# A hybrid decoder trunk on one core: another place for the powers, the weights' copies and the third value chunk

## The chip, the cores and the metric

The kernel runs on one core of a Trainium2 chip. The metric is the device time of one execution in microseconds. The core has five engines that run their own instruction streams and meet only at semaphores: TensorE (PE, with its weight loads as PEld), VectorE (DVE), ScalarE (ACT), GpSimd (POOL) and SyncE (SP). Each engine executes its stream in the order in which it is written; a wait stands for all that is behind it on that engine.

## The reference, cut to what matters

One inference step of a two-layer trunk for a prompt of 512 tokens and 8 sample tokens. Around the change lies layer 0's mixer. It has three computations side by side:

```python
# samples: attention over 4096 paged past positions each, k and v gathered by page table
a = softmax(q1 @ k1 * s + bias) - lam * softmax(q2 @ k2 * s + bias);  out = a @ v
# prompt: the same with a causal mask, 4 heads, blocks of 128 queries
# prompt and samples: gated linear attention, in chunks of C = 16 tokens
att = where(causal, qe @ ke.T, 0);  o = att @ v + qe @ S
S = exp(b_last) * S + kd.T @ v
# each head's output
o = o * rsqrt(mean(o * o) + eps) * g          # times silu(gate) for the linear heads
```

Then the output projection, an MLP, layer 1 (a gated recurrent block) and its MLP follow, all dense products.

## The kernel before

**Stages.** 13 chunks of the input projection; then 16 attention units (head, query block) of the prompt; then 8 GLA units (token block `tb`, pair of heads `hp`), numbered `u` in the loops of lines 1455 (VectorE), 965 (ScalarE) and 1923 (TensorE); then the projections and MLPs in `products` (line 1710).

**The paged cache.** The samples' keys and values come in 128 gathers (64 for k, 64 for v) of 1 MB, all issued by GpSimd with `indirect_dma_start` (line 705) into a ring of six buffers `KV`. `ORDER` fixes their order: 28 of k, then `v k v` per attention unit, then `k v` three times per GLA unit 0 to 5, so that key steps 44 + 3u to 46 + 3u and value chunks 32 + 3u to 34 + 3u belong to GLA unit u (units 6 and 7 have key steps 62 and 63 only). Before GpSimd issues gather i it goes through what belongs to gather i - 6, whose buffer it takes: it makes the product of the key step one ahead (`pool_product`), and waits in `release` until that buffer's user is done.

**A key step.** Half of it is VectorE's (`k_first`, lines 1247 and 1249: product and reduction into `SC`), half is GpSimd's product into the one buffer `PROD[:, 1]` (line 638), which VectorE reduces in `k_second` (line 1235). `k_chunks` on VectorE does `k_second(n - 1)` and then `k_first(n)`; the product of step n waits for `k_second(n - 1)`:

```python
            if n >= 1:
                po.wait_ge(prod1_used, n)
```

At the last step of a sample (n % 8 == 7) its own `k_second(n)` follows at once.

**A value chunk.** TensorE (`v_chunks`, line 1870) multiplies it with `PM`, a copy of the softmax weights that GpSimd makes (`weights`, line 651; the first also clears the tile, line 646). One copy serves four chunks: chunk n needs copy n // 4.

**The norm of an output.** When the outputs of unit u are in `OT`, VectorE clamps them (`clamp`, line 1415), ScalarE sums the squares, GpSimd takes the power -1/2 (`power`, lines 662 and 666), VectorE multiplies (`inverse_norm`, line 1421), ScalarE makes a diagonal of it (line 911), TensorE multiplies with it (`normalise`, line 1885) and ScalarE evicts (line 917). In the GLA loop all that from the power on stands in the next unit: unit u normalises the outputs of u - 1, counted as 15 + u. `POWERS_BEFORE_K` says before the product of which key step a power stands on GpSimd, `POWER_BEHIND_V` behind the release of which value chunk.

**A GLA unit.** TensorE: transpose (line 1927), masks' products (line 1933, which wait for the clamp), a value chunk, updates (line 1945), a second chunk, the sample's outer product, `normalise`, a third chunk, outputs (lines 1961 and 1966), which wait for the eviction of `normalise`. VectorE: a key step, masks (line 1462), eight state updates (line 1467), `inverse_norm`, a key step, `state_write` (line 1392), a key step, the clamp.

Of the kernel before, what the change touches and what calls it, by code (L numbers as in the profile page):

```python
# [112 lines left out]
def trunk(nc, ctx, a, o):  # L113
# [56 lines left out]
    RING = len(KV)  # L170
# [120 lines left out]
    def sem(name):  # L291
        return ctx.enter_context(nc.semaphore(name))
# [128 lines left out]
    v_used = sem("v_used")  # L421
# [75 lines left out]
    ORDER = load_order()  # L497
# [130 lines left out]
    def _(po):  # L628
# [25 lines left out]
        K_IN_UNITS = sum(UNIT_STEPS) + 2 * 11 + sum(PRE_STEPS)  # L654
        POWERS_BEFORE_K = {K_IN_UNITS: (14, 15), **{K_IN_UNITS + 3 * u + 1: (15 + u,) for u in range(1, 7)}}
        POWER_BEHIND_V = {**{2 * u + 1: u - 1 for u in range(1, 15)}, 53: 22, 57: 23}

# [10 lines left out]
        def release(i):  # L668
            kind, n = ORDER[i]
            if kind == "k":  # L670
                po.wait_ge(k_used, n + 1)
                po.wait_ge(prod1_ready, n + 1)
            else:
                po.wait_ge(v_used, n + 1)
                if n in POWER_BEHIND_V:
                    power(POWER_BEHIND_V[n])

        def weights_behind(i):

            kind, n = ORDER[i]  # L680
            if kind == "v":
                if n == 0:
                    weights(0)
                if n % 8 == 1:
                    weights(2 * (n // 8) + 1)
                if n % 8 == 7 and n < 63:
                    weights(2 * (n // 8) + 2)

        AHEAD = 1
        for i in range(LOADS + RING):  # L690
            if i >= RING:
                weights_behind(i - RING)
                for ahead in range(0 if i == RING else AHEAD, AHEAD + 1):
# [9 lines left out]
            if i < LOADS:  # L703
                kind, n = ORDER[i]
# [436 lines left out]
    def _(ve):  # L1141
# [313 lines left out]
        for u, (tb, hp) in enumerate(GLA_UNITS):  # L1455
            steps = GLA_STEPS[u]
# [7 lines left out]
            for n in range(8):  # L1464
                if n % 4 == 0:
                    ve.wait_ge(u_done, 2 * u + n // 4 + 1)
                V.scalar_tensor_tensor(ST[:, hp, state(tb, n + 1)], ST[:, hp, state(tb, n)], DECC[:, hp, 8 * tb + n:8 * tb + n + 1],  # L1467
                                       update(n, slice(0, P)), ALU.mult, ALU.add).then_inc(st_ready, 1)
                ve.wait_ge(st_ready, 8 * u + n + 1)
            if u:  # L1470
                inverse_norm(15 + u)
            k_chunks(min(max(steps - 1, 0), 1))
            state_write(u)
# [188 lines left out]
    def _(pe):  # L1662
# [260 lines left out]
        for u, (tb, hp) in enumerate(GLA_UNITS):  # L1923
# [26 lines left out]
            state_values(u)  # L1950
            pe.wait_ge(st_ready, 8 * u + 8)
            if u:
                normalise(15 + u)
            v_chunks(34 + 3 * u, 1)
            if u:
                pe.wait_ge(nev_done, outputs_done(16 + u))
# [128 lines left out]
```

## Time and profile before

| what | value |
|---|---|
| median of 3 runs | 1643.63 us (1642.11 to 1647.47) |
| the profiled execution, its own time | 1642.11 us |
| its span in the trace | 1640.3 us |
| PE, PEld busy | 88%, 79% |
| DVE, ACT, POOL busy | 56%, 30%, 21% |
| attention units (from the first value chunk) | 232 to 366 us |
| GLA units, transpose of the first to the last chunk's end | 381 to 543 us |

The profile is of one execution. The page gives shares over the whole span, and the stages differ: before 554 us the transfers, VectorE and GpSimd work most of the time, behind it TensorE nearly alone. So stretches are read by themselves: a window gives each engine's busy time in it, the granted clock of TensorE as a share of 2.4 GHz (PEclk) and the mean busy share of the 16 DMA engines. A timeline row gives start and duration, and in brackets how long the engine had been idle and what released it.

### The profile page before, as it was taken

To read this page: it belongs to the slowest core of one execution; us is meant where nothing else is said; L and a number is where in the kernel's file an instruction comes from. 1 tells how busy PE (TensorE), PEld (TensorE's weight loads), DVE (VectorE), ACT (ScalarE), POOL (GpSimd) and SP (SyncE) were. 2 spreads that over 40 slices of the span, in tenths; PEclk is the share of its full clock that TensorE was granted. 3 is DMA by queue.
4 is the path that set the end of the run, shared out by engine and by line. 5 is a ranking of instruction groups with operands and counts; after the bars stand their busy time and mean duration, and the time that the engine had idled before them with its cause. 6 is when DMAs were issued, how large, how long until landed. Compare 5 with 4: busy or idle time off the path is not lost.

```text
span 1640.3 us, 25826 instructions
## 1 busy us (share of the span) xinstructions
PE 1441.9 (88%) x11004; PEld 1291.3 (79%) x11004; DVE 912.9 (56%) x1157; ACT 499.9 (30%) x800; POOL 339.6 (21%) x270
## 2 busy tenths in 40 slices
PE   4999957767777788999999998799979999999995
PEld 3999823434333687999999997799969999999994
DVE  2498978766885527435353444769536434353433
ACT  3322354431322323212121223437243212121222
POOL 1085768865675000000000000002000000000000
PEclk9999979887777799999999999899989999999998
DMA  8477699996889431232322321112212232222311
GB/s 296 134 257 243 237 326 379 376 384 240 330 312 346 168 103 52 81 100 82 99 95 86 103 78 52 54 60 71 92 38 78 81 101 89 92 92 89 103 53 52
DMA packets 127892, 250.32 MB, mean 153 GB/s; under 512 B 5267, under 2 KB 108455, under 8 KB 111136
## 3 DMA queue, kind: packets, MB, share of 16 engines
q0 software_dynamic: 18432, 134.23, 21.5%
q1 hardware_dynamic: 101984, 105.00, 19.8%
q10 hardware_dynamic: 7368, 9.50, 1.8%
q8 instruction: 87, 1.43, 0.4%
q14 instruction: 21, 0.17, 0.0%
HBM read 241.04 MB, written 7.73 MB: 152 GB/s over the span
## 4 chain that ended last, share of the span: by engine, by line
PE 74%; DVE 13%; POOL 4%; ACT 4%; DMA 2%; issue 2%; ACTq 0%; another core or an unknown queue 0%; DVEq 0%; POOLq 0%
PE PS L1710 62%; PE PS L1695 3%; POOL PROD L638 3%; DMA KV<-in_cache_v,CIDX 2%; PE PS L1870 2%; DVE SC L1235 1%; DVE RS L1188 1%; POOL KV L705 1%; DVE TMP L1214 1%; PE PS L2003 1%; DVE ST L1467 1%; PE PS L1945 1%; DVE X L1218 1%; DVE ACC L1619 1%; DMA XSIN<-in_x_sample 1%
## 5 line engine op out<-in xcount | busy, mean ns | idle before, releaser
L1710 PE MATMUL PS<-H_hi,W_hi 128*128 128x260 f32 x1936 | 397.6, 287 | 23.2 <-DVE H_lo L1184 13.2
L1710 PE MATMUL PS<-H_hi,W_lo 128*128 128x260 f32 x1936 | 394.1, 286 | 0.0
L1710 PE MATMUL PS<-H_lo,W_hi 128*128 128x260 f32 x1936 | 393.4, 285 | 0.0
L1710 PEld LDWEIGHTS PS<-H_hi,W_hi 128*128 128x128 f32 x1936 | 304.1, 192 | 27.7 <-issue 20.6
L1710 PEld LDWEIGHTS PS<-H_hi,W_lo 128*128 128x128 f32 x1936 | 302.6, 191 | 0.0
L1710 PEld LDWEIGHTS PS<-H_lo,W_hi 128*128 128x128 f32 x1936 | 302.0, 191 | 0.0
L1179 DVE TENSOR_TENSOR W_lo<-RAW,W_hi 128x2048 fp32r<-128x2048 f32 x94 | 217.4, 2313 | 130.5 <-ACT W_hi L775 129.9
L775 ACT ACTIVATE W_hi<-RAW 128x2048 fp32r<-128x2048 f32 x94 | 179.5, 1909 | 278.0 <-PE PS L1710 277.7
L1710 PE MATMUL PS<-U_hi,W_lo 128*128 128x260 f32 x1024 | 206.4, 283 | 0.0
L1710 PE MATMUL PS<-U_lo,W_hi 128*128 128x260 f32 x1024 | 206.0, 283 | 0.0
L1710 PE MATMUL PS<-U_hi,W_hi 128*128 128x260 f32 x1024 | 206.0, 282 | 0.0
L638 POOL TENSOR_TENSOR PROD<-KV,QB 128x1024 f32<-128x1024 f32 x64 | 151.8, 2372 | 123.4 <-DVE SC L1235 91.7
L1710 PEld LDWEIGHTS PS<-U_hi,W_hi 128*128 128x128 f32 x1024 | 157.9, 188 | 0.0
L1710 PEld LDWEIGHTS PS<-U_hi,W_lo 128*128 128x128 f32 x1024 | 157.9, 188 | 0.0
L1710 PEld LDWEIGHTS PS<-U_lo,W_hi 128*128 128x128 f32 x1024 | 157.4, 188 | 0.0
L1574 DVE TENSOR_TENSOR ACC<-ACC,PS 128x520 f32<-128x520 f32 x64 | 44.6, 697 | 200.3 <-PE PS L1710 200.3
L1037 ACT ACTIVATE UF<-SQ 128x520 f32<-128x520 f32 x64 | 40.8, 638 | 279.9 <-DVE SQ L1564 279.9
L721 POOL TENSOR_TENSOR INP<-GX,ACC 128x520 f32<-128x520 f32 x7 | 14.5, 2081 | 505.6 <-ACT GX L1106 499.2
L1870 PE MATMUL PS<-KV,PM 128*32 128x512 f32 x512 | 87.0, 767 | 27.8 <-DMA KV<-in_cache_v,CIDX 15.7
L1564 DVE SCALAR_TENSOR_TENSOR SQ<-PS,RS 128x520 f32<-128x520 f32 x64 | 44.8, 700 | 112.9 <-PE PS L1710 112.9
L1695 PE MATMUL PS<-SQ,ONES 128*128 128x260 f32 x256 | 72.9, 442 | 33.3 <-ACT SQ L797 33.3
L1695 PEld LDWEIGHTS PS<-SQ,ONES 128*128 128x128 f32 x256 | 51.9, 218 | 53.3 <-issue 29.0
(287 smaller groups left out, 1509.1 us busy)
## 6 DMA issues: line engine op xcount, KB each, us to landing
RAW<-in_w_up SPq DMA_DIRECT2D x32, 1024.0 KB
RAW<-in_w_down SPq DMA_DIRECT2D x32, 1024.0 KB
RAW<-in_w_in_even SPq DMA_DIRECT2D x13, 1024.0 KB
RAW<-in_w_in_odd SPq DMA_DIRECT2D x8, 1024.0 KB
RAW<-in_w_out_odd SPq DMA_DIRECT2D x5, 1024.0 KB
RAW<-in_w_out_even SPq DMA_DIRECT2D x4, 1024.0 KB
x_saved<-X ACTq DMA_DIRECT2D x1, 2080.0 KB, 6.4
X<-x_saved SPq DMA_DIRECT2D x1, 2080.0 KB, 9.4
```

What stands on the lines that cost most here:

```text
L638: nc.gpsimd.tensor_tensor(PROD[:, 1], KV[i % RING][:, 2:4, :], QB[:, None, b % 2, :].to_broadcast([P, 2, 512]), ALU.mult).then_inc(prod1_r ...
L705: po.indirect_dma_start(KV[i % RING].rearrange("p n f -> p (n f)"), None, cache[kind], bass.IndirectOffsetOnAxis(ap=CIDX[:, n:n + 1], axis ...
L775: A(W_hi[:, ch.slot], RAW[:, ch.slot], ACT.Copy).then_inc(w_hi_ready, 1)
L1037: A(UF[:, i], RL[:, i], ACT.Square).then_inc(uf_ready, 1)
L1179: V.tensor_tensor(W_lo[:, ch.slot], RAW[:, ch.slot], W_hi[:, ch.slot].bitcast(F32), ALU.subtract).then_inc(w_lo_ready, 1)
L1188: V.reciprocal(RS[:, 1], RS[:, 0]).then_inc(inverse_ready, 1)
L1214: t = V.scalar_tensor_tensor(TMP[:, q], ACC[:, kt + q], VEC[:, gain + kt + q:gain + kt + q + 1], RS[:, 1], ALU.mult, ALU.mult)
L1564: V.scalar_tensor_tensor(pair(RL[:, i]), banks(ch.par[i]), 0.0, pair(RS[:, 1]), ALU.max, ALU.mult).then_inc(banks_free[ch.par[i]], 1)
L1574: V.tensor_tensor(pair(ACC[:, m]), pair(ACC[:, m]), banks(ch.par[i]), ALU.add).then_inc(banks_free[ch.par[i]], 1)
L1695: t = MM_(PS[:, 4 + i, 0:HALF], ONES[:], SQ[:, kt % 2, half], start=kt == 0, stop=kt == KT - 1)
L1710: t = MM_(PS[:, 2 * ch.par[i] + j, 0:HALF], w[:, ch.slot, k, cols], x[:, k, half], start=k == 0 and n == 0, stop=k == KT - 1 and n == 2)
L1870: t = MM_(PS[32 * pos:32 * pos + 32, 4, :], PM[:, part % 2, at:at + 32], KV[i % RING][:, pos, :], start=n % 32 == 0, stop=n % 32 == 31)
```

## The change

On GpSimd the weights' copies move from ahead of the product that is one step ahead to behind it, directly ahead of the wait for the value chunk (`weights_behind` goes into `release`). The powers of the GLA units move from before key step 45 + 3u to before key step 46 + 3u (`3 * u + 2`), and the last ones behind other value chunks: 21 from key step 63 to chunk 51, 22 from chunk 53 to chunk 54. On VectorE the middle key step of a GLA unit comes before `inverse_norm`. On TensorE the third value chunk of a GLA unit comes before `normalise`. No instruction is added or removed.

```diff
--- before.py
+++ after.py
@@ -652,8 +652,8 @@
                                   SC[b % SLOTS][:, :, 16 * half:16 * half + 16].rearrange("p j n -> p n j")).then_inc(pm_ready, 1)
 
         K_IN_UNITS = sum(UNIT_STEPS) + 2 * 11 + sum(PRE_STEPS)
-        POWERS_BEFORE_K = {K_IN_UNITS: (14, 15), **{K_IN_UNITS + 3 * u + 1: (15 + u,) for u in range(1, 7)}}
-        POWER_BEHIND_V = {**{2 * u + 1: u - 1 for u in range(1, 15)}, 53: 22, 57: 23}
+        POWERS_BEFORE_K = {K_IN_UNITS: (14, 15), **{K_IN_UNITS + 3 * u + 2: (15 + u,) for u in range(1, 6)}}
+        POWER_BEHIND_V = {**{2 * u + 1: u - 1 for u in range(1, 15)}, 51: 21, 54: 22, 57: 23}
 
         def power(u):
 
@@ -671,25 +671,19 @@
                 po.wait_ge(k_used, n + 1)
                 po.wait_ge(prod1_ready, n + 1)
             else:
-                po.wait_ge(v_used, n + 1)
-                if n in POWER_BEHIND_V:
-                    power(POWER_BEHIND_V[n])
-
-        def weights_behind(i):
-
-            kind, n = ORDER[i]
-            if kind == "v":
                 if n == 0:
                     weights(0)
                 if n % 8 == 1:
                     weights(2 * (n // 8) + 1)
                 if n % 8 == 7 and n < 63:
                     weights(2 * (n // 8) + 2)
+                po.wait_ge(v_used, n + 1)
+                if n in POWER_BEHIND_V:
+                    power(POWER_BEHIND_V[n])
 
         AHEAD = 1
         for i in range(LOADS + RING):
             if i >= RING:
-                weights_behind(i - RING)
                 for ahead in range(0 if i == RING else AHEAD, AHEAD + 1):
                     j = i - RING + ahead
                     if j < LOADS and ORDER[j][0] == "k":
@@ -1467,9 +1461,9 @@
                 V.scalar_tensor_tensor(ST[:, hp, state(tb, n + 1)], ST[:, hp, state(tb, n)], DECC[:, hp, 8 * tb + n:8 * tb + n + 1],
                                        update(n, slice(0, P)), ALU.mult, ALU.add).then_inc(st_ready, 1)
                 ve.wait_ge(st_ready, 8 * u + n + 1)
+            k_chunks(min(max(steps - 1, 0), 1))
             if u:
                 inverse_norm(15 + u)
-            k_chunks(min(max(steps - 1, 0), 1))
             state_write(u)
             slot(GLA_SLOT + 2 * u + 1)
             k_chunks(max(steps - 2, 0))
@@ -1949,10 +1943,9 @@
             v_chunks(33 + 3 * u, 1)
             state_values(u)
             pe.wait_ge(st_ready, 8 * u + 8)
+            v_chunks(34 + 3 * u, 1)
             if u:
                 normalise(15 + u)
-            v_chunks(34 + 3 * u, 1)
-            if u:
                 pe.wait_ge(nev_done, outputs_done(16 + u))
             for par in range(2):
                 h, rows = 2 * hp + par, slice(64 * par, 64 * par + 64)
```

Line 655's dictionary holds, before: `{44: (14, 15), 48: (16,), 51: (17,), 54: (18,), 57: (19,), 60: (20,), 63: (21,)}`; after: `{44: (14, 15), 49: (16,), 52: (17,), 55: (18,), 58: (19,), 61: (20,)}`. GpSimd's stream in GLA unit 2, with the wait for a buffer's user left out: before, power 17, product 51, gathers v41 and k54, copy 10, product 52, gathers v42 and k55; after, product 51, gathers v41 and k54, power 17, product 52, copy 10, gathers v42 and k55. The copies that end up behind a product are 0, 8, 9, 10, 11, 12 and 13.

## Rows read from the trace of the kernel before

**Rows 1.** The chain that ended last: start us, us, what.
```profile
553.99 49.02 PE PS L1710 x384
```

**Rows 2.** Busy time by window: attention's end, then two units of line 1927.
```profile
310.00:350.00 40.00, 33.23 (x189) 15.05 (x188) 32.58 (x52) 16.76 (x56) 30.95 (x32) 0.86 0.96 386
...
417.20:438.05 20.85, 13.89 (x108) 7.13 (x105) 16.53 (x27) 8.51 (x23) 16.02 (x15) 0.69 0.85 312
438.05:453.03 14.98, 11.26 (x107) 5.72 (x103) 12.24 (x23) 5.04 (x19) 9.27 (x9) 0.89 0.78 299
```

**Rows 3.** Waits from 372 to 556 us: total, times, longest.
```profile
POOL PROD L638 <- DVE SC L1235: 35.7, 12, 14.7
...
DVE NRS L1421 <- POOL NRS L666: 4.4, 1, 4.4
```

**Rows 4.** Timeline of unit 2: start us, us, engine, line, tiles, idle before.
```profile
424.80 0.72 POOL L666 TENSOR_TENSOR NRS<-NRT,EPSC 128x2 f32<-128x2 f32 x1
...
426.72 1.21 DVE L1235 TENSOR_REDUCE SC<-PROD 128x16 f32<-128x1024 f32 x1
...
428.08 2.36 POOL L638 TENSOR_TENSOR PROD<-KV,QB 128x1024 f32<-128x1024 f32 x1 [2.56 <-DVE SC L1235]
...
430.35 1.44 DVE L1392 SCALAR_TENSOR_TENSOR S<-PS,KSS,S 64x128 f32<-64x128 f32 x4
...
431.93 0.94 POOL L705 DMA_INDIRECT KV<-in_cache_k,CIDX  x1 [0.30 <-issue]
...
432.88 0.41 POOL L651 COPY PM<-SC 128x128 f32<-128x128 f32 x1
...
433.43 1.94 PE L1870 MATMUL PS<-KV,PM 128*32 128x512 f32 x8 [5.29 <-POOL PM L651]
...
435.30 0.80 PE L1961 MATMUL PS<-GVT,ATTM 128*128 128x128 f32 x2
...
439.21 0.42 DVE L1415 TENSOR_SCALAR OTC<-PS 128x256 f32<-128x256 f32 x1 [3.33 <-ACT OT L983]
```

**Rows 5.** Timeline of units 1, 3, 6 and 7, single steps.
```profile
411.80 1.93 PE L1870 MATMUL PS<-KV,PM 128*32 128x512 f32 x8 [0.79 <-DMA KV<-in_cache_v,CIDX]
...
447.90 1.21 DVE L1235 TENSOR_REDUCE SC<-PROD 128x16 f32<-128x1024 f32 x1
...
503.61 1.21 DVE L1235 TENSOR_REDUCE SC<-PROD 128x16 f32<-128x1024 f32 x1
...
508.55 0.53 PE L1961 MATMUL PS<-GVT,ATTM 128*128 128x128 f32 x2
...
522.14 0.16 DVE L1421 SCALAR_TENSOR_TENSOR NRS<-NSQ,NRS 128x2 f32<-128x2 f32 x1
...
522.88 0.69 PE L1885 MATMUL PS<-NDG,OT 128*128 128x128 f32 x4 [0.62 <-ACT NDG L911]
...
524.50 0.49 PE L1961 MATMUL PS<-GVT,ATTM 128*128 128x128 f32 x2
```

**Rows 6.** Timeline of unit 0, single steps.
```profile
381.73 1.93 PE L1870 MATMUL PS<-KV,PM 128*32 128x512 f32 x8
...
383.59 1.98 PE L1945 MATMUL PS<-GVT,KDM 128*64 128x128 f32 x16
...
384.08 2.35 POOL L638 TENSOR_TENSOR PROD<-KV,QB 128x1024 f32<-128x1024 f32 x1 [14.68 <-DVE SC L1235]
...
386.75 3.02 DVE L1467 SCALAR_TENSOR_TENSOR ST<-ST,DECC,PS 128x128 f32<-128x128 f32 x8
```

**Rows 7.** Timeline of the first attention unit, single steps.
```profile
230.62 1.02 POOL L646 MEMSET PM<- 128x1072 f32 x1
...
232.24 1.94 PE L1870 MATMUL PS<-KV,PM 128*32 128x512 f32 x8 [1.74 <-POOL PM L651]
...
234.72 2.37 POOL L638 TENSOR_TENSOR PROD<-KV,QB 128x1024 f32<-128x1024 f32 x1 [2.62 <-DVE SC L1235]
...
237.24 1.02 POOL L705 DMA_INDIRECT KV<-in_cache_v,CIDX  x1 [0.15 <-POOL PROD L638]
```

## The prediction

> **What bounds the kernel now.** I read the page first: the program's end is set by TensorE for most of the span, so an edit counts only if it lengthens or shortens a stretch in which the dense products (line 1710) wait for something. The edit touches only the stretch before the output projection, which follows at 553.99 us of the span [rows 1]. So I cut that stretch into its units with the windows view, one window from each transpose of line 1927 to the next. In a unit no engine is full: in the unit of 20.85 us VectorE works 16.53, GpSimd 16.02, TensorE 13.89 and the transfers 0.85 of the time; in the next, of 14.98 us, it is 12.24, 9.27, 11.26 and 0.78 [rows 2]. Work of 12 to 17 us on each of four resources fills units of 15 to 22 us: the stage is bound by the order in which they hand over to one another, and a reordering can cost much without adding any work. The waits view says which hand-over matters: GpSimd's product waits 35.7 us for VectorE's second reduction of the step before, and VectorE waits for GpSimd's power once only, 4.4 us [rows 3]. The timeline of one unit then gives each step of the loop; in it the third chunk of values waits 5.29 us for the copy of the weights [rows 4].
>
> **The change part by part.** It adds and removes no instruction. It moves three things: on GpSimd the power of a unit goes behind one more product and pair of gathers, and the weights' copy goes behind the product ahead of it; on VectorE the middle key step goes ahead of `inverse_norm`; on TensorE the third chunk of values goes ahead of `normalise`. What matters is who waits for whom in the new order.
>
> *The power.* Take the unit of rows 4 and call t0 the end of its middle `k_second` (426.72 + 1.21 = 427.93). Now the power is over at 425.52 (424.80 + 0.72), and `inverse_norm` runs just ahead of 426.72 without waiting. After the change VectorE does the key step first and comes to `inverse_norm` where it now comes to the state write, 2.42 us after t0 (430.35). GpSimd may start its product only 0.15 after t0 (428.08), then takes 2.36 for it, issues two gathers and is free at 432.87, 4.95 after t0; only there will the power stand. It is the 0.72 and a small operation ahead of it, which I take at 0.3 (the copy, which is larger, takes 0.41): 1.0 us. So `inverse_norm` runs 6.1 us after t0, and VectorE stands for 3.7 us. The stall isn't covered: behind it are the state write (1.44) and the third `k_second`, which alone lets GpSimd start its next product. That product starts now at t0 + 5.6 at the earliest; it will start at about 6.1 + 0.1 + 1.5 + 1.2 + 0.15 = t0 + 9.1.
>
> *The rest of the loop.* From `inverse_norm` over the diagonal, the normalising matmuls and their eviction to the outputs it is 2.4 us (522.14 to 524.50), of which 1.6 are from those matmuls on (522.88) [rows 5]. The outputs' start to the clamp is 3.9 us (435.30 to 439.21), and from the clamp over the next unit's masks, first chunk, updates and states to its middle `k_second` 8.7 (439.21 to 447.90), which takes 1.2. So t0 to the next t0 is 6.1 + 2.4 + 3.9 + 8.7 + 1.2 = 22.3 us, if no transfer is later than that. That `k_second` stands now at 447.90 and, three units on, at 503.61: 18.6 us a unit [rows 5]. **Units 3, 4 and 5 cost 3.7 us each, 11.1 together.** In unit 1 the outputs now stand straight behind the third chunk, which waits for its gather (411.80, for 1.93). That gather goes out 0.5 later still than the unit, since the copy of this unit (0.41) stands behind a product as well; behind the chunk there will be matmuls and eviction of `normalise` (1.6), and I add 0.3 for the Silu that ScalarE does ahead of it: **2.4 us.** In unit 6 the power stands behind the product of step 63, its gathers and chunk 51, so `inverse_norm` is at t0 + 6.1 there too (VectorE, which has another `k_second` ahead, stands 2.3), and the outputs at t0 + 8.5; they are now at 508.55, 3.7 after its t0 of 504.82. That is 4.8, and 2.3 if the outputs wait for something else now: **4.0 us**, near the upper one, since TensorE has nothing else there. Unit 7: the power waits for chunk 54 instead of 53, 0 to 1.1 us (a chunk at the upper clock level): **0.6 us.**
>
> *The weights.* The chunks of values of one part cannot start before the part's copy (0.41). In the unit of rows 4 the copy stands at 432.88 and the third chunk (433.43) already waits for it. After the change, ahead of it stand the power and the next product, and that product waits for the third `k_second`: t0 + 9.1, with a row sum 0.4 more, + 2.36 for the product, and the copy is over at t0 + 12.4, at 440.3. The chunk starts 7 us later than now, and since `normalise` will stand behind it on TensorE, the outputs follow 1.9 + 1.6 us after it: t0 + 15.9 where a unit with the stall alone has them at 8.5. The next t0 comes at t0 + 15.9 + 3.9 + 8.7 + 1.2 = 29.7, against 21.2 now (447.90 minus 426.72). **Unit 2 costs 8.5 us.** In unit 5 the copy stands behind a product as well, but there it only moves a chunk that ends before the power, so I add nothing. In unit 0, the first chunk of values, 381.73 now, goes ahead of all update matmuls; its copy gets behind the product at 384.08, which ends at 386.44. The chunk starts at 387.0 in place of 381.73 (5.3 late), the updates behind it at 389.0, and the states after the first half of them (1.98), at 391.0 and not at 386.75 [rows 6]: **4.3 us.** Ahead of that, the power of unit 14 no longer stands behind a copy, **0.5 us less**. At the first unit of attention the same happens with the memset (1.02) and the first copy: the product runs at 234.72 to 237.09, so chunk 0 starts at 238.7, not 232.24, and the gather that waits for it goes out at about 240.8, not 237.24 [rows 7]. 6.5 us late on TensorE, 3.5 on the transfers. From 310 to 350 us the transfers are 0.96 busy [rows 2], so they can win back little; of the bounds 0 (all won back) and 6.5 I take **3.0 us**, near the gather's delay.
>
> Sum: 3.0 - 0.5 + 4.3 + 2.4 + 8.5 + 11.1 + 4.0 + 0.6 = 33.4 us. Against the profiled execution's own 1642.1 us (span 1640.3) this is 1675.5. The median shown, 1643.6, is 1.5 higher; a median run would be at 1677, and I take 1676 between them.
>
> *The clock.* In the short unit, at a granted clock of 0.89, most matmuls run at the upper of the two levels (2.4 GHz); at 0.69 many run at the lower (1.2 GHz) [rows 2], and a chunk of values then takes 1.94 [rows 4]. If TensorE waits longer per unit, it may stay at the lower level in units that are now at the upper. By rows, at most 3 us in unit 3 and 1 in others; it widens the upper end by 6 us and isn't in the sum. The Trainium skill ("TensorE: Matmul & The Clock Gate", Part 1: The HAM clock gate) says that the throttled state is the default and that activity releases it; the trace agrees, with 0.69 in the unit in which TensorE is busy 13.89 of 20.85 us and 0.89 in that with 11.26 of 14.98. By the rule the sum would lie up to those 6 us higher.
>
> **The rivals.** (a) *The transfers are the bound and swallow most of it.* The gather engine keeps a rate, the ring of six buffers stays full, and a late instruction only eats waiting. For it: 0.96 busy in attention. Against it: 0.85 and 0.78 in these units, and each gather is issued behind the very product that now starts 3.5 us later. If half of the delays in units 0 to 7 (30.9 us) were swallowed, and all of attention's, it would be 1642.1 + 15.5 - 0.5 = 1657. (b) *Faster.* `k_second` goes ahead of `inverse_norm` and the product ahead of the copy, so GpSimd is let go earlier, and the third chunk no longer waits for the diagonal; its buffer is refilled sooner. The gain per unit is at most 0.16 (`inverse_norm`), 0.5 (copy) and 1.2 (`normalise`, where the values have landed): some 5 us over the stage, 1637. It decides if the power is there when VectorE asks for it: GpSimd would have to be 3.7 us further ahead than t0 allows, that is to have begun the product before the `k_second` that frees its buffer. I see no row for that. (c) *Nothing moves:* the stalls just replace other waits of the same engines; VectorE idles 4.3 us in the unit of 20.85, about one stall. But its idle time there is the wait for the outputs at the unit's end, which gets later too. 1642. (d) *More than the sum:* each delay also runs at the lower clock, and attention's 6.5 us stays whole: 33.4 + 3.5 + 6, about 1685.
> The Trainium skill ("DMA: Bandwidth & Descriptors", Anatomy of one DMA) gives for one gather of 1 MiB through GpSimd's path an estimate of 2.0 us plus its bytes at 436 GB/s, 4.4 us. No row here shows a gather by itself, and if that held for the later-spaced gathers, the 0.5 us in unit 1 would vanish, 33.4 becoming 32.9; nothing else here uses it.
>
> **How the numbers follow.** Forecast (1664 to 1683) 0.67, (a) 0.14, (d) 0.10, (c) 0.04, (b) 0.05. A measurement of this kernel can tell about 0.3%, 5 us, from no change. Slower by more than that: 0.91; within: 0.04; faster: 0.05. The range takes in (a) and (d): 1655 to 1689.
>
> **What would show it.** In the trace after: VectorE waiting for GpSimd's power (line 666) at `inverse_norm` in five or six units, some 3.5 us each, where it is one wait of 4.4 us now; the third `k_second` of a unit 5 us or more behind the middle one's key step; in unit 2 a chunk of values waiting over 7 us for PM; in unit 0 TensorE waiting about 5 us for PM; at attention's start about 6 us for the same; the units from transpose to transpose at 22 us in place of 18.7; nothing changed from the output projection on but its start. I am wrong if the power stands ready at `inverse_norm`, or if the units keep their length although VectorE stalls, which would say that the transfers or TensorE set it.

## The result: 2.6% slower, 42 us

Timed side by side on one chip, the changed kernel takes 1686.57 us (median of 4 runs, 1682.45 to 1688.24) and the one before 1642.87 (4 runs, 1641.93 to 1647.47). The ratio is 1.0256 with a 95% interval of 1.0229 to 1.0285: 42.1 us slower, 37.6 to 46.8. (This ratio is an estimate over all runs and not the quotient of the two medians, which lie 43.7 us apart.) I had forecast 1676.0, that is 33.4 us more; the range of 1655 to 1689 holds the time, the narrower 1664 to 1683 of the forecast itself does not. The profiled execution of the changed kernel took 1682.64 us with a span of 1680.8, 40.5 us more span than before. Sums below are made against those 40.5 us.

In the changed kernel the lines behind 692 have numbers lower by 6, and behind 1955 by 7 (the chunks of values are 1864, the dense products 1704, the outputs 1954). In the runs further down they are off by one or a few as well.

First the page of the kernel after, its span and busy times:

```profile
span 1680.8 us, 25820 instructions
...
PE 1455.7 (87%) x11004; PEld 1298.4 (77%) x11004; DVE 913.1 (54%) x1157; ACT 500.1 (30%) x800; POOL 339.4 (20%) x270
```

VectorE, ScalarE and GpSimd are as busy as before within 0.3 us each (912.9, 499.9 and 339.6 us there): no work came in. TensorE has 13.8 us more than before's 1441.9 although it runs the same matmuls. I come back to that.

The chain that ended last says that the whole loss lies ahead of the output projection, whose products start 40.6 us later than in [rows 1]. Columns are start us, us, what:

```profile
564.75 10.44 DMA out_gla_prompt<-ST
...
594.57 48.98 PE PS L1704 x384
```

The waits view of the kernel after, from 372 to 596 us, answers to [rows 3]; columns are total us, times, longest:

```profile
POOL PROD L638 <- DVE SC L1229: 64.3, 17, 14.7
...
DVE NRS L1415 <- POOL NRS L666: 24.3, 8, 4.7
...
PE PS L1864 <- POOL PM L651: 20.7, 3, 13.5
```

VectorE's one wait of 4.4 us for the power, which is that for the last power, behind unit 7, has become eight, 24.3 us together: that one is still there with 4.7, units 1 to 6 have 1.15, 3.68, 4.06, 3.67, 4.60 and 2.16, and unit 7 has 0.33. GpSimd's product, which waited 35.7 us for VectorE, waits 64.3: the stall of the one is handed on to the other. And the three chunks of values that waited 7.6 us for a copy of the weights before wait 20.7.

The timeline of unit 2 after shows both in one unit. It answers to [rows 4]; a number in brackets is the idle time of that engine ahead of the instruction, and who ended it:

```profile
440.18 1.22 DVE L1229 TENSOR_REDUCE SC<-PROD 128x16 f32<-128x1024 f32 x1
...
441.54 2.35 POOL L638 TENSOR_TENSOR PROD<-KV,QB 128x1024 f32<-128x1024 f32 x1 [3.41 <-DVE SC L1229]
...
446.62 0.73 POOL L666 TENSOR_TENSOR NRS<-NRT,EPSC 128x2 f32<-128x2 f32 x1
447.45 0.16 DVE L1415 SCALAR_TENSOR_TENSOR NRS<-NSQ,NRS 128x2 f32<-128x2 f32 x1 [3.68 <-POOL NRS L666]
...
450.69 2.35 POOL L638 TENSOR_TENSOR PROD<-KV,QB 128x1024 f32<-128x1024 f32 x1 [3.35 <-DVE SC L1229]
...
452.99 0.39 POOL L651 COPY PM<-SC 128x128 f32<-128x128 f32 x1
...
453.52 1.94 PE L1864 MATMUL PS<-KV,PM 128*32 128x512 f32 x8 [13.55 <-POOL PM L651]
...
455.39 1.23 PE L1879 MATMUL PS<-NDG,OT 128*128 128x128 f32 x4
...
457.33 0.49 PE L1954 MATMUL PS<-GVT,ATTM 128*128 128x128 f32 x2 [0.71 <-ACT PJ L911]
```

Read it from t0 = 440.18 + 1.22 = 441.40, the end of the middle `k_second`. GpSimd's product, which that step lets go, and its two gathers keep it until 446.3; the power follows; `inverse_norm` runs at t0 + 6.05 after a stall of 3.68. The next product starts at t0 + 9.3, the copy ends at t0 + 12.0, and TensorE, which has stood for 13.55 us, starts the chunk at t0 + 12.1 and the outputs at t0 + 15.9. The prediction had 6.1 for `inverse_norm`, 3.7 for the stall, 9.1 for the product, 12.4 for the end of the copy and 15.9 for the outputs.

To add up the loss I cut both traces at the masks' products (line 1933 before, 1927 after), at whose start the outputs of the unit before are over. Two of the units, first before and then after. Columns are the window, its length, busy us (instructions) of TensorE, its weight load, VectorE, ScalarE, GpSimd, then the granted clock, the transfers' share and GB/s:

```profile
399.30:418.30 19.00, 15.58 (x107) 7.32 (x107) 16.94 (x30) 5.29 (x17) 14.17 (x12) 0.68 0.98 373
...
476.20:494.80 18.60, 14.80 (x105) 7.68 (x105) 16.45 (x28) 6.28 (x21) 14.03 (x13) 0.68 0.87 324
```

```profile
409.40:432.30 22.90, 19.84 (x107) 8.92 (x107) 16.87 (x30) 5.13 (x15) 15.74 (x13) 0.50 0.83 318
...
504.90:529.90 25.00, 17.80 (x105) 8.91 (x106) 16.50 (x28) 6.30 (x22) 15.13 (x13) 0.57 0.73 258
```

These are units 1 and 5. Such cuts for all of the stage give what each part lost, beside its term of the forecast. "Before" and "after" are lengths in us. One trace is one execution, so the last column gives the same stretch in other traces: those of the six runs below that move one copy, one clearing or one gather of the kernel before (`e5` to `e8`, `e10`, `e11`), each where it leaves the stretch alone.

| stretch | before | after | more | forecast | unchanged, elsewhere |
|---|---|---|---|---|---|
| start of chunk 0 (after: less its added wait) | 232.2 | 231.6 | -0.7 | none | 229.2 to 233.7 |
| chunk 0 to unit 0 (after: with the added wait, 6.4) | 148.8 | 155.4 | +6.6 | +3.0, -0.5 | 147.9 to 150.0 |
| unit 0 | 18.3 | 22.5 | +4.3 | +4.3 | 18.3 to 19.0 |
| unit 1 | 19.0 | 22.8 | +3.8 | +2.4 | 19.4 to 21.7 |
| unit 2 | 21.5 | 28.2 | +6.7 | +8.5 | 20.7 to 21.8 |
| unit 3 | 18.7 | 22.0 | +3.3 | +3.7 | 18.2 to 18.7 |
| unit 4 | 17.6 | 22.4 | +4.8 | +3.7 | 17.1 to 17.8 |
| unit 5 | 18.7 | 25.0 | +6.3 | +3.7 | 18.5 to 19.0 |
| unit 6 | 19.2 | 22.1 | +2.9 | +4.0 | 15.3 to 16.2 |
| unit 7 to the output projection | 39.9 | 42.5 | +2.6 | +0.6 | 38.2 to 40.0 |
| sum | | | +40.6 | +33.4 | |

The first line is no effect of the change, which does nothing ahead of chunk 0 but delay it: that start varies by more from run to run. Unit 6 of the kernel before is 3 us longer in this trace than in any of the others. ScalarE's second copy of its outputs stands there for something that the profile can't name:

```profile
513.19 0.28 ACT L983 ACTIVATE OT<-PS 128x128 f32<-128x128 f32 x1 [1.94 <-remote]
```

Against the other traces unit 6 loses about 6 us, not 2.9, and unit 1 about 2.5, not 3.8. The terms that are most short are attention, unit 5, what follows unit 6 and, by this better base, unit 6 itself.

What follows unit 6 has a wait that the kernel before doesn't have in this trace. ScalarE sends the last states out (`out_gla_prompt`) and may begin the split of the output projection's input (`H_hi`) only when they have landed. First before, then after:

```profile
534.15 2.18 ACT L998 ACTIVATE H_hi<-PJ 128x512 fp32r<-128x512 f32 x4
```

```profile
575.21 2.19 ACT L992 ACTIVATE H_hi<-PJ 128x512 fp32r<-128x512 f32 x4 [2.89 <-DMA out_gla_prompt<-ST]
```

That is the transfer of 10.44 us in the chain above, and its 2.89 us are about the 2.6 of the table.

### The profile page after: what moved, and what is told of

It reads as the page before. It is cut to its first block, busy times and chain, and to the rows that moved or that the text cites. A ratio compares the mean times of both kernels' runs of the same rounds, so it can differ in the third digit from the quotient of the medians.

```text
span 1680.8 us, 25820 instructions
## 1 busy us (share of the span) xinstructions
PE 1455.7 (87%) x11004; PEld 1298.4 (77%) x11004; DVE 913.1 (54%) x1157; ACT 500.1 (30%) x800; POOL 339.4 (20%) x270
## 3 DMA queue, kind: packets, MB, share of 16 engines
q1 hardware_dynamic: 101984, 105.00, 19.4%
## 4 chain that ended last, share of the span: by engine, by line
PE 74%; DVE 13%; ACT 4%; POOL 4%; issue 2%; DMA 2%; ACTq 0%; DVEq 0%; POOLq 0%
PE PS L1704 61%; PE PS L1689 3%; POOL PROD L638 3%; PE PS L1864 2%; DVE SC L1229 2%; DVE RS L1182 1%; PE PS L1939 1%; DVE TMP L1208 1%; PE PS L1996 1%; POOL KV L699 1%; DVE ST L1461 1%; DVE X L1212 1%; DVE ACC L1613 1%; PE PS L1959 1%; DMA out_gla_prompt<-ST 1%
## 5 line engine op out<-in xcount | busy, mean ns | idle before, releaser
L1864 PE MATMUL PS<-KV,PM 128*32 128x512 f32 x512 | 90.7, 797 | 45.1 <-POOL PM L651 28.9
```

What stands on the lines that cost most here:

```text
L1864: t = MM_(PS[32 * pos:32 * pos + 32, 4, :], PM[:, part % 2, at:at + 32], KV[i % RING][:, pos, :], start=n % 32 == 0, stop=n % 32 == 31)
```

## The experiments

My theory after the result: the three moves cost what the hand-over loop says, the first copy costs its whole delay since nothing wins back transfer time that is lost in attention, and the copy of unit 5, which I had put at nothing, costs something. The rivals: the transfers take part of it up (then attention's share is under 6), the chunk order is what hurts, or the lower clock carries what is missing. "Ratio" is against the kernel before in the same batch, with a 95% interval; each is turned into us with that batch's median of before (1642.9, 1640.0 or 1639.3; the batches ran on different chips). A difference of medians can be some us off from it: 9.6 in place of 12.2 for `e3_chunk`, 24.6 in place of 26.4 for `e9_early_powers`. Lengths of units are from the one trace of each run, cut as above.

### The three moves, each alone

**All copies late, all else as before (`e1_copies`).**

```diff
             else:
+                weights_behind(i, True)
                 po.wait_ge(v_used, n + 1)
...
-                weights_behind(i - RING)
+                weights_behind(i - RING, False)
```

> Only the weights' copies go behind the product; powers, VectorE and TensorE keep their order. Theory (the loop of hand-overs sets the stage, late work ahead of a value chunk is paid in full): copy 0 costs 6.5 us, copy 8 costs 3.8, copy 10 about 3 (it stands behind product 52, 433.5 to 435.9, so the chunk starts at 436.4 and not 433.4), copy 12 about 3: some 16 us, 1659. Rival (the gathers' rate sets it, late instructions are mostly swallowed): under 6 us.

Measured: 1658.82 us, ratio 1.0091 (1.0071 to 1.0112), 15.0 us more, beside the theory's 16. Its unit 2, TensorE:

```profile
453.14 1.94 PE L1871 MATMUL PS<-KV,PM 128*32 128x512 f32 x8 [8.28 <-POOL PM L651]
455.01 0.80 PE L1962 MATMUL PS<-GVT,ATTM 128*128 128x128 f32 x2
```

The chunk's wait is 8.28 instead of 5.29 us [rows 4], and the outputs stand straight behind it.

**All powers late (`e2_powers`).** The two tables of the change and VectorE's order; TensorE and the copies as before.

```diff
-        POWERS_BEFORE_K = {K_IN_UNITS: (14, 15), **{K_IN_UNITS + 3 * u + 1: (15 + u,) for u in range(1, 7)}}
-        POWER_BEHIND_V = {**{2 * u + 1: u - 1 for u in range(1, 15)}, 53: 22, 57: 23}
+        POWERS_BEFORE_K = {K_IN_UNITS: (14, 15), **{K_IN_UNITS + 3 * u + 2: (15 + u,) for u in range(1, 6)}}
+        POWER_BEHIND_V = {**{2 * u + 1: u - 1 for u in range(1, 15)}, 51: 21, 54: 22, 57: 23}
...
+            k_chunks(min(max(steps - 1, 0), 1))
             if u:
                 inverse_norm(15 + u)
-            k_chunks(min(max(steps - 1, 0), 1))
```

> Only the powers go one product and two gathers later and VectorE's middle key step goes ahead of inverse_norm (the two can't be parted: the late power alone would wait for a key step that stands behind it). Theory: inverse_norm waits 3.7 us in units 2 to 5, 1 in unit 1, 2.3 in unit 6, and TensorE's third chunk, still behind normalise, adds 1 us a unit: 20 to 25 us, 1662 to 1668. Rival (gathers): under 10 us.

Measured: 1673.1 us, ratio 1.0185 (1.0164 to 1.0207), 30.4 us more (26.9 to 34.0): above the 20 to 25 that I expected. Its waits view from 372 to 596 us:

```profile
POOL PROD L638 <- DVE SC L1235: 56.0, 15, 14.7
...
DVE NRS L1421 <- POOL NRS L666: 24.2, 8, 4.5
```

The stalls for the power are those of the whole change (24.2 against 24.3 us), so the moved power makes them. VectorE's order, moved with it here, doesn't: `e9_early_powers` below has that order with early powers, and none of these stalls.

**The third chunk ahead of `normalise` (`e3_chunk`).**

```diff
+            v_chunks(34 + 3 * u, 1)
             if u:
                 normalise(15 + u)
-            v_chunks(34 + 3 * u, 1)
-            if u:
                 pe.wait_ge(nev_done, outputs_done(16 + u))
```

> Only TensorE's third chunk goes ahead of normalise. Theory: the norm is not the late one before, the chunk is (its gather or its copy), so the order costs the matmuls and the eviction of normalise behind the chunk, 1 to 1.6 us in the four or five units in which the chunk waits for a gather or copy: plus 4 to 7 us, 1647 to 1650. Rival (the buffer is let go earlier and that is what counts): minus 2 to 5 us.

Measured: 1652.51 us (6 runs, 1645.63 to 1657.13), ratio 1.0074 (1.0054 to 1.0093), 12.2 us more (8.9 to 15.3). The rival that expected a gain falls, and the loss is larger than the theory had. The profiled execution is the fastest of the six (1645.63), so its timeline can't show the median's loss; it shows the mechanism. Unit 2, TensorE and the clamp:

```profile
434.31 1.93 PE L1870 MATMUL PS<-KV,PM 128*32 128x512 f32 x8 [6.38 <-POOL PM L651]
436.17 1.22 PE L1885 MATMUL PS<-NDG,OT 128*128 128x128 f32 x4
...
438.11 0.80 PE L1960 MATMUL PS<-GVT,ATTM 128*128 128x128 f32 x2 [0.72 <-ACT PJ L917]
...
442.17 0.42 DVE L1415 TENSOR_SCALAR OTC<-PS 128x256 f32<-128x256 f32 x1 [5.40 <-ACT OT L983]
```

`normalise` could run while TensorE waits for the copy. Behind the chunk, it and ScalarE's eviction lie on the way to the outputs: 438.11 - 436.17 = 1.9 us.

**The power and the chunk together (`e4_no_copies`),** the change without its copies.

> The change without its copies: powers, VectorE's and TensorE's order as in the kernel after, copies ahead of the product as before. Theory (parts add up, but the order of chunk and normalise costs nothing once the norm is late): 42 us of the whole less 6.5 for copy 0, 4.3 for copy 8, 4.8 for copy 10 in the presence of the late power (8.5 less 3.7) and 2.5 for copy 12: 24 us, 1667. Rival (copies are cheap, the powers carry nearly all): 35 us, 1678.

Measured: 1671.91 us, ratio 1.0176 (1.0159 to 1.0193), 28.9 us more. That lies between the theory's 24 and the rival's 35. With the late power the chunk order costs nothing more that could be measured (30.4 without it), whereas alone it costs 12.2. Where the power is late, the chunk can run in the time in which TensorE waits for it anyway. And 28.9 + 15.0 (the copies alone) = 43.9, beside 42.1 for the whole: copies on one side, power and chunk on the other, add up within their intervals.

**The change with early powers (`e9_early_powers`):** the two tables put back, everything else as in the change.

> The kernel after with the powers alone back where they were; copies, VectorE's and TensorE's order stay changed. Theory (the late power is the stall, not VectorE's new order): inverse_norm waits for no power in units 1 to 6, and what is left is the copies' 15 and the chunk order's 10 us: plus 25, 1665 to 1668. Rival (VectorE's order itself costs, the norm coming one key step later): over 32, 1675.

Measured: 1663.93 us, ratio 1.0161 (1.0132 to 1.019), 26.4 us more. That is the theory's 25. VectorE waits for a power once again, 4.4 us, as before. Undoing the power's move gives back 16 us, though that move alone costs 30. So "what the power costs" has no single value: taken first it is 30, taken last it is 16. The order in which the parts are taken says why: the copies cost 15.0, the chunk order (with VectorE's) on top of them 26.4 - 15.0 = 11.4, about what it costs alone, and the power on top of both 15.7. A late power hides the chunk order, so whichever comes first has the whole of the shared part.

### The copies one by one

Each runs one copy in the changed place, all else as before.

```diff
+        LATE = (0,)          # or (8,), (10,), (12,)
...
+                if part is not None and (part in LATE) == late:
+                    weights(part)
```

> Only copy 0 and the clearing of its tile go behind product 28. Theory (nothing of it is won back, since attention's next product waits for VectorE, which waits for TensorE): the first chunk 6.5 us late and the whole 6.5 later, 1649.5. What the prediction took (the transfers win part of it back): 3.0. Rival (the gathers' rate alone counts): 3.6, the delay of the next gather.

> Only copy 8 goes behind product 44. Theory: unit 0 is 4.3 us longer and power 14 0.5 us earlier, 3.8 in all, 1646.7. Rival (transfers, which are only half busy in this unit, catch up in unit 1): under 1 us.

> Only copy 10 goes behind product 52. Theory: the third chunk of unit 2 starts at 436.4 and not 433.4 and unit 2 is 3 us longer: 1646. In the kernel after, with the late power, the same copy cost more because its product waits for the third k_second. Rival: the copy is no longer the late one here, 0.

> Only copy 12 goes behind product 60. The prediction took nothing for it. By the trace of the kernel after, the chunk behind it waited 5.85 us for it, and by the order of the loop the outer product and the state write stand behind that chunk: plus 3 us, 1643 to 1646 beside a kernel before of 1640 to 1643. Rival (the prediction's): 0.

| copy | of | us | ratio | more | chunk's wait, before | with this copy late | its unit: elsewhere, here, in `e1` |
|---|---|---|---|---|---|---|---|
| 0 | attention | 1646.86 | 1.0040 (1.0022 to 1.0057) | 6.6 | 1.74 | 8.10 | see below |
| 8 | unit 0 | 1644.91 | 1.0031 (1.0012 to 1.0051) | 5.1 | none | 5.07 | 18.3 to 19.0, 22.2, 22.3 |
| 10 | unit 2 | 1643.68 | 1.0025 (1.0009 to 1.0041) | 4.1 | 5.29 | 8.29 | 20.7 to 21.8, 24.8, 24.7 |
| 12 | unit 5 | 1646.45 | 1.0043 (1.0027 to 1.0059) | 7.0 | 1.00 | 5.95 | 18.5 to 19.0, 23.4, 23.3 |

The two columns of waits are the idle time in brackets at that chunk. What is added to it (6.4, 5.1, 3.0 and 5.0 us) is near the price for each of the four. The four come to 22.8 us singly and 15.0 together, but each has an interval of some 3 us to either side, so this doesn't show that they hide one another. The traces say that they don't: each unit is as long with its copy late alone as in `e1_copies`, where all are late.

*Copy 0* costs 6.6 us. The prediction gave 3.0, with 6.5 as the upper bound. *Copy 12* costs 7.0 where the prediction gave nothing, which is more than the 3 I expected of this run too (its interval is 4.4 to 9.7). Its unit 5, first in the kernel before and then with only this copy late:

```profile
482.80 0.40 POOL L651 COPY PM<-SC 128x128 f32<-128x128 f32 x1
...
483.35 1.06 PE L1870 MATMUL PS<-KV,PM 128*32 128x512 f32 x8 [1.00 <-POOL PM L651]
484.35 1.12 PE L1847 MATMUL PS<-GVTOK,CONST 8*128 8x512 f32 x2
...
488.30 1.94 PE L1870 MATMUL PS<-KV,PM 128*32 128x512 f32 x8 [1.88 <-DMA KV<-in_cache_v,CIDX]
...
494.83 0.89 PE L1933 MATMUL PS<-QE,KE 64*128 64x128 f32 x4 [0.68 <-DVE OTC L1415]
```

```profile
489.98 2.35 POOL L638 TENSOR_TENSOR PROD<-KV,QB 128x1024 f32<-128x1024 f32 x1 [2.68 <-DVE SC L1236]
...
492.28 0.39 POOL L651 COPY PM<-SC 128x128 f32<-128x128 f32 x1
...
492.81 1.94 PE L1871 MATMUL PS<-KV,PM 128*32 128x512 f32 x8 [5.95 <-POOL PM L651]
494.68 2.07 PE L1848 MATMUL PS<-GVTOK,CONST 8*128 8x512 f32 x2
...
496.86 0.34 DVE L1393 SCALAR_TENSOR_TENSOR S<-PS,KSS,S 64x128 f32<-64x128 f32 x1 [4.64 <-PE PS L1848]
...
503.02 0.58 PE L1934 MATMUL PS<-QE,KE 64*128 64x128 f32 x4 [0.79 <-DVE OTC L1416]
```

The chunk isn't the last of its kind here: behind it on TensorE is the product of line 1848, which VectorE's state write waits for (4.64 us), with the next `k_second` behind that. I had looked only at the chunk's end against the power's. The two matmul groups also take longer: behind the 5.95 us of idle time they run at the lower level of the clock, 1.94 and 2.07 us in place of 1.06 and 1.12. It is tempting to add these 1.83 us to the added wait of 4.95 and find the 7.0. The trace doesn't bear that out: unit 5 is 23.4 us long in it and 18.7 in the kernel before, 4.8 us more (23.45 - 18.67) and not 6.8. From this chunk to the masks of the next unit it is 11.5 us before (494.83 - 483.35) and 10.2 here (503.02 - 492.81), since the third chunk waited 1.88 us for its gather before and doesn't now. So the copy costs its added wait, and the rest of the 7.0 is within the run's interval.

### Can attention win transfers back?

**GpSimd 3.7 us late from one gather on (`e11_gather_late`).** GpSimd clears a spare tile 18 times ahead of the gather of chunk 4, the one that copy 0 delays; copy 0, power and orders stay.

```diff
+        DUMMIES = 18
...
+                if (kind, n) == ("v", 4):
+                    for j in range(DUMMIES):
+                        nc.gpsimd.memset(DUM[:, :], 0.0).then_inc(pm_zeroed, 1)
+                        po.wait_ge(pm_zeroed, j + 2)
```

> The kernel before with 18 small clearings of a spare tile on GpSimd ahead of the gather of chunk 4, the first behind product 28: they should take some 2 to 5 us (read from the trace), so that gather and all behind it on GpSimd goes out that much later, while chunk 0 starts in time. Theory (in attention the hand-overs set the pace, but the gathers at 0.94 to 0.99 busy leave no room for winning back): between half and all of the delay stays at the end. Rival (the gathers wait in the ring anyway): nothing stays.

GpSimd's timeline, the delay and the gather behind it:

```profile
238.47 3.69 POOL L709 MEMSET DUM<- 128x64 f32 x18
242.43 1.01 POOL L711 DMA_INDIRECT KV<-in_cache_v,CIDX  x1 [0.27 <-POOL DUM L709]
```

Measured: 1644.52 us, ratio 1.0027 (1.0011 to 1.0043), 4.4 us more, 1.8 to 7.1. Against the delay of 3.7 us this leaves nothing that was won back, though the interval allows half of it. The traces are sharper. From the start of chunk 0 to the masks of unit 0 it is 147.9 to 150.1 us in the seven traces that have copy 0 early and all gathers in time (148.9 on average), 147.8 to 150.2 in the five in which chunk 0 starts 6.4 us late (148.6), and 152.7 in this one. So the first 6.4 us are there at the end in full, and so are these 3.7. The windows of the first attention stretch and of a later one, before and then after:

```profile
228.00:248.00 20.00, 14.26 (x82) 6.36 (x83) 16.85 (x27) 8.34 (x26) 15.30 (x16) 0.81 0.99 345
```

```profile
228.00:248.00 20.00, 11.15 (x60) 4.76 (x60) 10.54 (x17) 7.25 (x23) 9.41 (x10) 0.65 0.82 284
...
310.00:350.00 40.00, 31.33 (x173) 14.31 (x169) 31.72 (x50) 16.73 (x58) 30.80 (x33) 0.83 0.98 380
```

The transfers fall from 0.99 to 0.82 busy while the first chunk is awaited, and from 310 us on they are at 0.98 as they were at 0.96 [rows 2]. So they are nearly full either way and have little room to make up for a pause. That this is the cause isn't shown apart from the hand-overs: in `e11_gather_late` the product behind is late as well, 10.1 us behind the one ahead of it and not 6.5, and no run delays the transfers alone.

### Does the clock carry the rest?

TensorE is busy 118.4 us in the units after and 109.3 before (sum of the eight windows up to 15 us into unit 7), for the same matmuls, at a granted clock of 0.50 to 0.68 in units 1 to 6 against 0.68 to 0.79. In unit 1 it is 19.84 of 22.90 us at 0.50 against 15.58 of 19.00 at 0.68. Part of that is spread between executions: in the six runs that move one thing the same sum is 106.1 to 113.5 us, and unit 1, untouched, is at 0.50 in `e8_copy12` too. Still, 118.4 is above all of them, and this looks like rival (d). To test it I gave TensorE idle matmuls in the changed kernel, into a part of PSUM that nothing reads in this stage, ahead of and behind the third chunk of units 2, 3, 4 and 6 (**`e12_warm`**, 50 in all):

```diff
+            warm({2: 20, 3: 5, 4: 5}.get(u, 0))
             v_chunks(34 + 3 * u, 1)
+            warm({3: 4, 4: 4, 6: 12}.get(u, 0))
...
+                MM_(PS[:, 3, 0:P], IDENT, IDENT, start=True, stop=True)
```

> The kernel after with idle matmuls (identity by identity into a free bank, results unused) where TensorE stood waiting in units 2, 3, 4 and 6: 20 and 5 and 5 ahead of the third chunk, 4, 4 and 12 behind it. They give TensorE work only, none of it needed. Theory (the 7 us that the parts' sum leaves open are matmuls at the lower clock): the granted clock of those units rises from 0.65 towards 0.9, and the time falls by 4 to 8 us against the kernel after, to 1679 to 1683. Rival (the clock plays no part on the path): same or, where the added matmuls outlast the wait, 1 to 4 us slower, 1687 to 1691.

Measured: 1684.87 us, ratio 1.0283 (1.026 to 1.0306), beside 1.0256 (1.0229 to 1.0285) for the change itself: no gain, at best a tie, and between what the theory and the rival had. The trace says that this wasn't the test that I meant. TensorE in its unit 2, the idle matmuls (with two records for each), the third chunk and the outputs:

```profile
442.38 4.73 PE L1884 MATMUL PS<-CONST 128*128 128x128 f32 x40
455.11 1.93 PE L1864 MATMUL PS<-KV,PM 128*32 128x512 f32 x8 [8.00 <-POOL PM L651]
...
458.91 0.79 PE L1961 MATMUL PS<-GVT,ATTM 128*128 128x128 f32 x2 [0.71 <-ACT PJ L911]
```

The idle matmuls are over 8.00 us before the chunk, which runs at the lower level of the clock all the same; so do the outputs, 0.79 us where the change alone had 0.49. In units 3 and 4 TensorE stands 3.62 and 2.58 us between the last idle matmul and `normalise`, and the outputs are at 0.79 us too. By unit, with the granted clock of each:

| unit | idle matmuls | the change: us, clock | with them: us, clock |
|---|---|---|---|
| 0 | none | 22.5, 0.65 | 22.3, 0.73 |
| 1 | none | 22.8, 0.50 | 24.4, 0.57 |
| 2 | 20 | 28.2, 0.68 | 30.3, 0.67 |
| 3 | 9 | 22.0, 0.66 | 22.5, 0.73 |
| 4 | 9 | 22.4, 0.65 | 22.1, 0.73 |
| 5 | none | 25.0, 0.57 | 24.4, 0.64 |
| 6 | 12 | 22.1, 0.65 | 21.7, 0.74 |

The units without idle matmuls gained 0.07 to 0.08 as well, and unit 1, which has none, is 1.6 us longer. So neither the clock nor the times can be put down to the idle matmuls. The Trainium skill ("TensorE: Matmul & The Clock Gate", Part 1: The HAM clock gate) has activity release the throttle; this run neither bears that out nor speaks against it.

Two other runs say more. The windows of `e2_powers` and then of `e4_no_copies`, from the masks of unit 0 to 15 us into unit 7:

```profile
380.80:556.60 175.80, 111.62 (x839) 55.89 (x842) 122.96 (x206) 43.62 (x148) 99.26 (x85) 0.69 0.73 265
```

```profile
384.10:557.60 173.50, 121.10 (x839) 61.96 (x842) 122.93 (x206) 43.70 (x148) 99.44 (x85) 0.63 0.73 268
```

The second has TensorE busy 9.5 us longer for the same matmuls, at 0.63 and not 0.69, and is no longer for it: 1671.91 us beside 1673.10. What it is busy longer it stands less, 52.4 and not 64.2 us. One place where the clock is on the path is the outputs: from their start to the next unit's masks it is 4.6 us in the units of the changed kernel in which they run at the lower level and 3.1 in its unit 2, where they run at the upper one (460.47 - 457.33). But five of the eight units have them at the lower level after the change, and five before it. So I find no sign that the clock carries much of the loss; what its share is stays open.

### The other way round

If copy 0 with its clearing costs 6.6 us behind a product and copy 10 costs 4.1, the two waits that the kernel before still has for them, 1.74 [rows 7] and 5.29 us [rows 4], might be had as well. **`e10_early`** changes the kernel before: the tile is cleared ahead of product 25, and copy 10 goes out behind chunk 38 instead of 39.

```diff
+            if n == 25:
+                po.wait_ge(tiles_done, first_tile(C_OUT0))
+                nc.gpsimd.memset(PM[:], 0.0).then_inc(pm_zeroed, 1)
...
-                po.wait_ge(tiles_done, first_tile(C_OUT0))
-                nc.gpsimd.memset(PM[:], 0.0).then_inc(pm_zeroed, 1)
...
-                if n % 8 == 7 and n < 63:
+                if n == 38:
+                    weights(10)
+                if n % 8 == 7 and n < 63 and n != 39:
```

> The kernel before, pushed the other way: copy 10 goes one chunk earlier (behind chunk 38 and ahead of product 51, where GpSimd waited 2.6 us for VectorE), and the tile is cleared ahead of product 25, where GpSimd waited 6.7 us. Theory (lateness of a copy ahead of a waiting chunk counts in full, and so does earliness): 3 to 4 us in unit 2 and 1.0 at attention's start, 4 to 5 us faster. Rival (another wait takes the place, the gather or the third key step): under 1 us.

Measured: 1635.34 us (12 runs, 1632.8 to 1639.0), the kernel before beside it 1639.32 (20 runs), ratio 0.9975 (0.9961 to 0.9989), 4.1 us faster than before (1.8 to 6.4). Chunk 0, the copy of unit 2 and its third chunk:

```profile
227.76 1.94 PE L1873 MATMUL PS<-KV,PM 128*32 128x512 f32 x8 [0.69 <-POOL PM L652]
...
424.61 0.42 POOL L652 COPY PM<-SC 128x128 f32<-128x128 f32 x1
...
430.53 1.93 PE L1873 MATMUL PS<-KV,PM 128*32 128x512 f32 x8 [2.17 <-DMA KV<-in_cache_v,CIDX]
...
437.02 0.89 PE L1936 MATMUL PS<-QE,KE 64*128 64x128 f32 x4 [0.64 <-DVE OTC L1418]
```

The copy is over 5.5 us before the chunk, which now waits for its gather (2.17 us). Unit 2 runs from 418.74 to 437.02, 18.3 us instead of 21.5; that is 3.2 of the 4.1. Whether the clearing adds its 1 us isn't shown: chunk 0 waits 1.05 us less, but from it to unit 0 this trace has 152.0 us, more than in any of the twelve traces counted above. This version beats both kernels, by a margin that is small but measured.

## Why the prediction was right, and where it was short

The direction, the stage and the mechanism were right, and the total was 42.1 (37.6 to 46.8) against 33.4 us. The signs that it named are in the trace: the stalls at `inverse_norm`, 13.55 us for PM in unit 2, 5.07 in unit 0, 6.4 more at attention's start, units of 22 us, and a loss at the output projection (40.6) that is the loss of the whole (40.5).

- **The power: right in its working.** `inverse_norm` at t0 + 6.05 (6.1 said) after a stall of 3.68 (3.7); five of the units 1 to 6 stall 2.16 to 4.60 us, unit 1 less (1.15). The units 3, 4 and 6 are 22.0 to 22.4 us long where I had 22.3. What they lose depends on the base. My 18.6 was a mean over three units, and unit 4 was 17.6, so it loses 4.8.
- **Unit 6: under-priced, and by luck it doesn't look so.** I read its 4.0 from the one trace of the kernel before, in which it is 19.2 us; six other traces have 15.3 to 16.2, so its loss is about 6 us.
- **Unit 0: right,** 4.3 us, with the chunk starting after 5.07 us of idle (5.3 said). With copy 8 alone late the unit is 22.2 us, 3.2 to 3.9 more than in traces that leave it alone.
- **Unit 2: right in its steps, 1.8 too much in size** (6.7 against 8.5). The outputs came at t0 + 15.9 as said. I then added the way on to the next t0 and took 21.2 off as the unit before. From masks to masks it was 21.5 to 28.2.
- **Attention: "near the gather's delay" failed,** the step that gave 3.0 between 0 and 6.5. It is 6.6, by the trace and by copy 0 alone. I counted the delay of a gather (3.5) as the cost, since the transfers are the full resource. But the chunk is 6.4 late, and GpSimd's next product waits for VectorE, which waits for TensorE, so the gathers behind the first pair are as late as the chunk: that product starts at 247.22 after and at 241.19 before. The 0.5 for the power of unit 14 is too small to be seen in this stretch.
- **Unit 5: "so I add nothing" failed.** The copy lengthens the unit by 4.8 us alone, and the unit loses 6.3 instead of 3.7. What is behind the chunk is an outer product that the state write needs, then the third chunk, then `normalise`. After the change the third chunk ends 1.7 us behind `inverse_norm`, where in units 3, 4 and 6 TensorE stands ready. The late power alone makes the unit 23.6 us, the copy alone 23.4, both together 25.0, where it is 18.5 to 19.0 without either: a third of the delay is shared.
- **What follows unit 6** is 2.0 us more than said. I had nothing there but the power of unit 7. The trace has ScalarE waiting 2.89 us for the states to be stored. `e2_powers` and `e4_no_copies` have the same wait, 2.49 and 3.25 us, and stretches of 42.6 and 43.1; `e1_copies` and `e9_early_powers` don't, at 39.8 and 40.3. But `e12_warm`, which has the late powers, doesn't have it either (39.8), and `e6_copy8` has it, so why the store is late is open.
- **Unit 1** is 3.8 longer than in the trace before and about 2.5 longer than in the others (2.4 said). It is the one at a granted clock of 0.50.

**The rivals.** (a), the transfers swallow it, fell: 42 us and not 15, and nothing of a late chunk or a delayed gather was won back. (b), faster, fell: the chunk order alone costs 12.2 us. (c) fell with the 42. (d), "more than the sum, about 1685", is what was measured, and I had given it 0.10, against 0.67 for the 1664 to 1683 that the time missed. Its half on attention is shown. Its other half, the lower clock, is seen in the trace (TensorE 9.1 us longer busy for the same matmuls in the units), but no run shows that it costs time, and what it would have had to fill is units 5 and 6 and the wait for the store. So (d) has the right size in part by luck.

## What to carry over

On an engine that works in order, put what another engine is waiting for ahead of the work that itself waits. Count then what is queued behind the late instruction on each engine, not just the instruction: the power was 1 us of work and stalled VectorE 3.7 us in unit 2, and the copy of unit 5, 0.4 us of work, made its unit 4.8 us longer through an outer product right behind its chunk.

Costs of single edits that fill the same wait don't add: the chunk order is 12 us alone and nothing beside a late power, which is 30 us taken first and 16 taken last. The copies, which sit in different units, did add. Say which base a cost is against. And take the base from more than one trace: one unit of the one that I used was 3 us longer than elsewhere. In attention, with the transfers 0.96 busy, nothing of a pause was made up for, so bound a delay there by the whole of it.

## What I had not expected of the hardware

- How far the same order spreads: the chunk order alone covers 11.5 us in six runs (1645.63 to 1657.13), `e9_early_powers` 11.2 in four (1661.34 to 1672.56), and the kernel before 10.8 in 29 runs of one batch (1634.28 to 1645.03). I don't know why.
- TensorE took 9.1 us (8%) more for the same matmuls in the units, and the granted clock of a unit that nothing touches differs from trace to trace: unit 1 has 0.50 in `e8_copy12` and 0.75 in `e11_gather_late`.
- A lower clock behind a wait isn't always paid for: with copy 12 late, the two matmul groups behind the wait took 1.94 and 2.07 us in place of 1.06 and 1.12, and yet the unit was longer by less than the added wait.
- A store of 64 KB can hold up the next stage: it took 10.44 us with the transfers 0.98 busy, and ScalarE stood 2.89 us for it.
